# A two-layer decoder step on one core: row loads behind the barrier signal, an early gain load, and new orders on VectorE and TensorE

## What is computed

```
def rmsnorm(x, g):
    y = xf * lax.rsqrt(jnp.mean(xf * xf, axis=-1, keepdims=True) + RMS_EPS)
    return (y * g.astype(F32)).astype(x.dtype)
...
for layer in (0, 1):
    xp, xs = mixer(rmsnorm(xp, norm_mix[layer])), ...      # + residual
    xp = xp + hier_moe(rmsnorm(xp, norm_ffn[layer]), ...)  # y = sum of gate * expert(x) over two experts
    xs = xs + hier_moe(rmsnorm(xs, norm_ffn[layer]), ...)
y_prompt = rmsnorm(xp, norm_final)
y_sample = rmsnorm(xs, norm_final)
```

## Time and profile before

| | |
|---|---|
| median of the runs | 1451.35 us |
| the profiled execution's own time | 1448.17 us |
| its span, first to last instruction | 1446.4 us |
| mean granted TensorE clock | 0.943 |
| TensorE products busy | 1241.4 us, 86% |
| VectorE busy | 370.9 us, 26% |
| ScalarE busy | 246.5 us, 17% |
| GpSimd busy | 209.8 us, 15% |
| read from and written to HBM | 356.1 MB, 246 GB/s over the span |

### The profile page before, as it was taken

How to read it: one execution, slowest core, us unless ns; L and a number is a source line. 1 busy time by engine, 2 the same in 40 slices (tenths; PEclk the granted TensorE clock), 3 DMA queues, 4 the chain that set the end, 5 groups by cost and what they waited for, 6 DMA issues and landing times.

```text
span 1446.4 us, 16227 instructions
## 1 busy us (share of the span) xinstructions
PE 1241.4 (86%) x6273; PEld 658.5 (46%) x6273; DVE 370.9 (26%) x792; ACT 246.5 (17%) x571; POOL 209.8 (15%) x268
## 2 busy tenths in 40 slices
PE   6999998888789899877868999998879899878860
PEld 4765575556544533323324764445634533323320
DVE  4132003554310531111115400113610621111115
ACT  2000004653210301100003201014410301000001
POOL 2300002322200011111001000204810111111000
PEclk9999999999999999988998999999989999998985
DMA  8320524749957579999958130302156679999945
GB/s 278 100 49 18 214 106 140 215 150 351 359 201 301 225 267 418 419 420 420 414 222 285 59 113 8 131 0 82 45 205 279 240 283 420 419 419 419 415 182 182
DMA packets 104396, 342.58 MB, mean 237 GB/s; under 512 B 21534, under 2 KB 40162, under 8 KB 80506
## 3 DMA queue, kind: packets, MB, share of 16 engines
q1 hardware_dynamic: 89176, 305.47, 55.4%
q0 software_dynamic: 14848, 35.94, 6.9%
q10 hardware_dynamic: 290, 0.07, 0.0%
HBM read 320.08 MB, written 36.02 MB: 246 GB/s over the span
## 4 chain that ended last, share of the span: by engine, by line
PE 55%; SPq 16%; DMA 9%; DVE 8%; issue 4%; POOL 3%; ACT 3%; POOLq 2%; DVEq 0%; ACTq 0%
SPq L1037 10%; PE ps L1243 8%; PE ps L1747 8%; PE ps L1168 8%; SPq L1059 4%; PE ps L437 4%; DMA moe_gu<-in_moe_w_up 4%; PE ps L415 4%; PE ps L1698 4%; PE ps L1261 4%; DMA fox_arena<-in_cache_k 2%; PE ps L356 2%; DVE x L1582 1%; PE ps L695 1%; POOLq L340 1%
## 5 line engine op out<-in xcount | busy, mean ns | idle before, releaser
L1243 PE MATMUL ps<-moe_gu,rows 128*64 128x512 f32 x1024 | 246.7, 637 | 54.9 <-DMA moe_gu<-in_moe_w_up 51.6
L1243 PEld LDWEIGHTS ps<-moe_gu,rows 128*64 128x64 f32 x1024 | 81.7, 146 | 199.5 <-issue 191.8
L1747 PE MATMUL ps<-mwblk,turned 128*128 128x512 f32 x256 | 111.5, 593 | 2.2 <-DVE vaug L1938 1.5
L1168 PE MATMUL ps<-moe_gu,turned 128*128 128x512 f32 x256 | 110.3, 593 | 0.0
L1525 DVE TENSOR_TENSOR turned<-turned,ps 128x256 f32<-128x256 f32 x32 | 13.5, 421 | 305.5 <-ACT turned L1341 305.5
L1128 POOL DMA_INDIRECT expert_rows<-turned,moe_row x32 | 32.1, 1002 | 393.3 <-ACT turned L1351 385.7
L1261 PE MATMUL ps<-moe_wd,moe_rowsel 128*64 128x512 f32 x352 | 80.4, 598 | 2.3 <-ACT turned L1351 2.3
L1168 PEld LDWEIGHTS ps<-moe_gu,turned 128*128 128x128 f32 x256 | 48.6, 190 | 61.8 <-issue 61.0
L1747 PEld LDWEIGHTS ps<-mwblk,turned 128*128 128x128 f32 x256 | 48.0, 190 | 61.1 <-issue 57.4
L1341 ACT ACTIVATE turned<-ps 128x256 f32<-128x256 f32 x32 | 12.3, 383 | 302.5 <-PE ps L1243 302.5
L356 PE MATMUL ps<-turned,fox_arena 128*128 128x288 f32 x256 | 63.1, 407 | 0.0
(11 more groups left out here) (345 smaller groups left out, 1501.0 us busy)
## 6 DMA issues: line engine op xcount, KB each, us to landing
moe_gu<-in_moe_w_gate SPq DMA_DIRECT2D x56, 1024.0 KB, 22.1
moe_gu<-in_moe_w_up SPq DMA_DIRECT2D x56, 1024.0 KB, 23.9
moe_wd<-in_moe_w_down SPq DMA_DIRECT2D x44, 1024.0 KB, 23.2
rows<-in_moe_w_down SPq DMA_DIRECT2D x20, 1024.0 KB, 22.8
fox_arena<-in_cache_k SPq DMA_DIRECT2D x32, 512.0 KB, 7.9
fox_arena<-in_cache_v POOLq DMA_DIRECT2D x32, 512.0 KB, 9.5
fox_arena<-in_fox_w_in SPq DMA_DIRECT2D x6, 2048.0 KB, 10.3
mwblk<-in_mlstm_w_in SPq DMA_DIRECT2D x6, 2048.0 KB, 8.6
```

What stands on the lines that cost most here:

```text
L1168: mm = pe.matmul(ps[:, 2 * n + half, :], turned[:, c, n * P:(n + 1) * P], w[:, c, half * 512:half * 512 + 512], start=(c == 0), stop=(c == ...
L1243: mm = pe.matmul(ps[h, 2 + p % 2, :].rearrange("s (k f) -> s k f", k=2), xT[:, c, h], gu[s][:, half, :, c, :], start=(c == 0), stop=(c == ...
L1747: mm = pe.matmul(ps[:, m % 4, :], turned[:, c, n * P:(n + 1) * P], wblk[:, k % 3, c, :], start=(c == 0), stop=(c == KC - 1))
```

## The change

1. `scattered` becomes a semaphore outside the sets that are cleared, and SyncE's wait for it with the five row loads moves out of `sp_` into `late_`, which `run` calls after SyncE's drain and its increment of `together`, and before its wait for `cleared`.
2. The final gain is loaded by SyncE in layer 1's experts phase, after the last down weights and once pair 14's gate and up products are done, into a part of `gu[1]` that no row load writes. `finish` loads nothing; its VectorE waits for the gain first.
3. `aT` becomes two buffers by pair, and for the last pair TensorE does `turn_hidden(15)` ahead of `down(14)`, not after it.
4. `combine` issues one of its two instructions at a call, so that others can stand between. In the projection VectorE's order becomes the one in the diff, tile 3's and tile 4's adds being placed otherwise; in `finish` the mean of the tile before stands between the two adds.
5. TensorE in the projection issues seven idle products at the start in place of six, does `gates_half(0)` ahead of tile 3's flip as before, and puts tile 4's flip into the middle of `first_half(0)`.

```diff
-            aT = scratch[:, 0:2 * P].rearrange("p (m t) -> p m t", t=P)
+            aT = [scratch[:, k * 2 * P:(k + 1) * 2 * P].rearrange("p (m t) -> p m t", t=P) for k in range(2)]
...
+            last_gain.append(gu[1][:].rearrange("p h k c n -> p (h k c n)")[:, 2 * D:3 * D])
...
+                if layer == 1:
+                    sp.wait_ge(gu_done, STATIC - 1)
+                    sp.dma_start(last_gain[1], i["norm_final"].rearrange("(a d) -> a d", a=1).broadcast_to([P, D])).then_inc(gl_in, 16)
...
+            def late_(sp):
                 sp.wait_ge(scattered, 1)
                 for n in range(NT):
                     sp.dma_start(held[n][0:ROWS[n], :], y_dram[2 * n * P:2 * (n * P + ROWS[n]), :].rearrange("(p j) d -> p (j d)", j=2)
...
+                    if p == STATIC - 1:
+                        pe.wait_ge(at_kept, p)
+                        pe.wait_ge(a_ready, p + 1)
+                        turn_hidden(pe, p)
...
-                    pe.wait_ge(a_ready, p + 1)
-                    turn_hidden(pe, p)
+                    if p < STATIC - 1:
+                        pe.wait_ge(a_ready, p + 1)
+                        turn_hidden(pe, p)
...
             def pe_(pe):
-                idle_products(pe, 6, 5)
...
+                idle_products(pe, 7, 5)
+                for n in range(3):
+                    flip(pe, n)
+                    idle_products(pe, 1, 5)
+                pe.wait_ge(wg_in, 80)
+                pe.wait_ge(gained, 3)
+                gates_half(pe, 0)
+                flip(pe, 3)
+                pe.wait_ge(w_in[0], 16)
+                first_half(pe, 0, range(0, KC // 2))
+                flip(pe, L)
+                first_half(pe, 0, range(KC // 2, KC))
                 pe.wait_ge(gained, NT)
                 gates_half(pe, 1)
-                first_half(pe, 1)
+                first_half(pe, 1, range(KC))
...
+                for n in range(2):
+                    add_rows(n, 0)
+                    add_rows(n, 1)
                 mean(0)
-                combine(dve, 0, 2, combined)
+                add_rows(2, 0)
+                add_rows(2, 1)
                 mean(1)
+                add_rows(3, 0)
+                mean(2)
                 keep(0)
-                combine(dve, 0, 3, combined)
-                mean(2)
+                add_rows(3, 1)
                 keep(1)
                 mean(3)
                 keep(2)
-                combine(dve, 0, 4, combined)
+                add_rows(4, 0)
+                add_rows(4, 1)
                 keep(3)
...
             def dve_(dve):
+                dve.wait_ge(gl_in, 16)
                 for n in range(NT):
-                    combine(dve, 1, n, combined)
+                    combine(dve, 1, n, 0, combined)
                     if n:
                         mean(dve, n - 1)
-                    if n == 0:
-                        dve.wait_ge(gl_in, 16)
-                    else:
+                    combine(dve, 1, n, 1, combined)
+                    if n:
                         end(dve, n - 1)
...
                     eng.drain().then_inc(together, 1)
+                    if who == "sp" and "late" in phase:
+                        phase["late"](eng)
                     eng.wait_ge(cleared, n + 1)
```

More of the change, by code:

```diff
@@ L185, in trunk @@
         back = []
+        gl_in, last_gain = lasting("gl_in"), []
         def idle_products(pe, count, bank):
@@ L1260, in down @@
                             h = slice(half * SLOT, (half + 1) * SLOT)
-                            mm = pe.matmul(ps[h, 5 + n, :], aT[:, m, h], wd[s][:, half, m, n * 512:(n + 1) * 512],
+                            mm = pe.matmul(ps[h, 5 + n, :], aT[p % 2][:, m, h], wd[s][:, half, m, n * 512:(n + 1) * 512],
                                            start=(m == 0), stop=(m == 1))
@@ L1345, in keep_hidden @@
                 act.wait_ge(at_done, p + 1)
-                act.activation(aT[:], ps[:, 4, 0:2 * P].rearrange("p (m t) -> p m t", t=P), ACT.Copy).then_inc(at_kept, 1)
+                act.activation(aT[p % 2], ps[:, 4, 0:2 * P].rearrange("p (m t) -> p m t", t=P), ACT.Copy).then_inc(at_kept, 1)
             def keep_rows_act(act, p, s):
@@ L1567, in dve_, with combine @@
                             keep_rows_dve(dve, p, 0)
-            phases.append(dict(sp=sp_, pool=pool_, pe=pe_, act=act_, dve=dve_, clears="act"))
+            phases.append(dict(sp=sp_, pool=pool_, pe=pe_, act=act_, dve=dve_, clears="act", late=late_))
             mx.close()
-        def combine(dve, layer, n, combined):
+        def combine(dve, layer, n, j, combined):
             r = ROWS[n]
-            dve.wait_ge(back_in[layer][n], 16)
-            for j in range(2):
-                if j:
-                    dve.wait_ge(combined, 2 * n + 1)
-                dve.scalar_tensor_tensor(x[0:r, n, :], back[layer][n][0:r, j * D:(j + 1) * D], share[j][0:r, n:n + 1], x[0:r, n, :], ALU.mult, ALU.add
-                                         ).then_inc(combined, 1)
+            if j:
+                dve.wait_ge(combined, 2 * n + 1)
+            else:
+                dve.wait_ge(back_in[layer][n], 16)
+            dve.scalar_tensor_tensor(x[0:r, n, :], back[layer][n][0:r, j * D:(j + 1) * D], share[j][0:r, n:n + 1], x[0:r, n, :], ALU.mult, ALU.add
+                                     ).then_inc(combined, 1)
         def mlstm_project(qT, kT, knat, vaug, og, nat, carryb, C, qs, ws, tri01, negg_dram, small):
@@ L1768, in gates_half, with first_half, flip @@
                     mm.then_inc(g_done, 1)
-            def first_half(pe, half):
-                for c in range(KC):
+            def first_half(pe, half, chunks):
+                for c in chunks:
                     mm = pe.matmul(ps[:, 4 + half, 0:HT], wblk[:, 0, c, 0:P], turned[:, c, half * HT:(half + 1) * HT],
                                    start=(c == 0), stop=(c == KC - 1))
-                if half:
+                if half and c == KC - 1:
                     mm.then_inc(k_done, 1)
-            def pe_(pe):
-                idle_products(pe, 6, 5)
-                for n, r in enumerate(ROWS):
-                    pe.wait_ge(scaled, n + 1)
-                    if n >= 2:
-                        pe.wait_ge(gained, n - 1)
-                    for c in range(KC):
-                        mm = pe.transpose(ps2[:, n % 2, c * P:c * P + r], rows[0:r, n, c:D:KC], ident[0:r, 0:r])
-                    mm.then_inc(flipped, 1)
-                    if n < 3:
-                        idle_products(pe, 1, 5)
-                    if n == 2:
-                        pe.wait_ge(wg_in, 80)
-                        pe.wait_ge(gained, 3)
-                        gates_half(pe, 0)
-                    if n == 3:
-                        pe.wait_ge(w_in[0], 16)
-                        first_half(pe, 0)
+            def flip(pe, n):
+                r = ROWS[n]
+                pe.wait_ge(scaled, n + 1)
+                if n >= 2:
+                    pe.wait_ge(gained, n - 1)
+                for c in range(KC):
+                    mm = pe.transpose(ps2[:, n % 2, c * P:c * P + r], rows[0:r, n, c:D:KC], ident[0:r, 0:r])
+                mm.then_inc(flipped, 1)
+            def pe_(pe):
+                idle_products(pe, 7, 5)
[10 more added lines that the diff above has]
+                first_half(pe, 0, range(KC // 2, KC))
                 pe.wait_ge(gained, NT)
                 gates_half(pe, 1)
-                first_half(pe, 1)
+                first_half(pe, 1, range(KC))
                 for g in range(1, 8):
@@ L2413, in finish @@
             L = NT - 1
-            sb("f_held", [P, 2 * NT, D], where=fin)
-            gl = sb("gl", [P, D], where=fin)
+            sb("f_held", [P, 2 * NT + 1, D], where=fin)
+            gl = last_gain[1]
             combined = sem("f_combined")
-            gl_in, squared, meaned, rooted, ended, y_out = (sem("gl_in"), sem("f_squared"), sem("f_meaned"), sem("f_rooted"),
+            squared, meaned, rooted, ended, y_out = (sem("f_squared"), sem("f_meaned"), sem("f_rooted"),
                                                             sem("f_ended"), sem("y_final"))
             def sp_(sp):
-                sp.dma_start(gl[:], i["norm_final"].rearrange("(a d) -> a d", a=1).broadcast_to([P, D])).then_inc(gl_in, 16)
                 for n in range(NT):
```

6 lines of the change are left out of this document (3 added, 3 removed).

## The result

The changed kernel took 1439.06 us (median of 20 runs, 1431.81 to 1448.98) against 1451.66 of the kernel before (20 runs, 1446.47 to 1458.44): 12.6 us less, a ratio of 0.9914 with a 95% interval of 0.9898 to 0.9930. The forecast was 15.2 less and 1436.2. Between executions of one kernel the time follows TensorE's clock: among these twenty the slowest had a mean granted clock of 0.937 and the fastest 0.948.

A forecast was written before the change was run, and what follows sets the result against it. Chains of waits at the experts' end, projection (TensorE) and last phase (the gain, then VectorE) bound it; 11.6 + 1.8 + 0.3 + 1.5 = 15.2 off the median 1451.35 gave 1436.2 us, own range 1433.5 to 1439, wide range 1431 to 1442.

The forecast's parts named there:

- The release: Barrier behind each layer's last scatter: signalling ahead of the row loads brings release 2.7 us behind the scatter, 3.1 earlier.
- rival B: Release doesn't move, because GpSimd's drain ends with something unseen: 1438.5 us, chance 0.08.
- The last phase, 11.6: Last phase: early release, early gain and means between adds end VectorE's work at 1431.4, saving 11.6 us.
- Four of these vanish, since the second add (1.28) now covers them: Last phase: four of five VectorE waits of 0.66 us for GpSimd's power disappear, 20.2 becoming 17.6.
- the sign of being right: Last phase: some 20.4 us from VectorE's first add to its last end, no idle time over 1 us.
- The last pair, 1.8 and 0.3: Experts' end: turning ahead of `down(14)` starts the last down products earlier, 1.8 us in layer 1, 0.3 in layer 0.
- The projection, 1.5: Projection behind layer 0: gate products start at 778.0, the phase ends 1.5 us earlier, bounds 0 and 3.2.
- The sum: Whole kernel: savings of 11.6, 1.8, 0.3 and 1.5 add up to 15.2 us.
- rival A: Layer 1's tail keeps its place through later pair 15 weights or a clock fall, losing the 1.8: 1438.0 us, chance 0.14.
- C: Last phase: row loads bound it, tiles 2 to 4 landing 3 to 4 us late: 1440 us, chance 0.05.
- E: DMA serves SyncE's waiting transfers side by side, delaying rows and last down weights: 6.4 us slower, 1457.8, chance 0.02.
- a sign of being wrong: Listed signs: rows releasing tiles 2 to 4, VectorE releasing a gate product, or GpSimd's drain over 3 us.

The follow-up runs named there:

- signal_last: The changed kernel with SyncE signalling the barrier after issuing the row loads, as before: 1441.24 us, ratio 0.9923 to the kernel before.
- adds_in_row: The changed kernel with both adds of a tile in a row in the last phase, the mean behind them: 1439.72 us, ratio 0.9911 to the kernel before.
- end_lagged: The changed kernel with each tile's end issued one tile later in the last phase: 1436.22 us, ratio 0.9894 to the kernel before.
- tail_filled: The changed kernel with the old projection order, last-phase ends one tile later, and one idle product on each side of the last turning: 1433.46 us, ratio 0.9870.
- bridged: The changed kernel with three idle products for one behind tile 2's flip and one ahead of tile 4's in the projection: 1437.55 us, ratio 0.9905.
- bridged_lagged: The changed kernel with bridged's extra idle products in the projection and last-phase ends issued one tile later: 1439.00 us, ratio 0.9922.
- gain_late: The changed kernel with the final gain loaded at the start of the last phase again: 1448.73 us, ratio 0.9974 to the kernel before.

## Why the prediction was right or wrong

The direction and the wide range (1431 to 1442) held; the size was 2.6 too large, and 1439.06 lies at the very edge of the forecast's own range, 1433.5 to 1439. That it came this near is in part luck, as errors of both signs add up below. By its own steps:

**The release.** Right. The drain behind layer 0's last scatter began at 757.21 and took 2.67; the rows' landings stayed (4.86 for tile 0). The last phase gains 1.7 us by it, where rival B's difference had been put at 2.0. In the projection nothing is shown to have been gained by it (signal_last).

**The last phase, 11.6.** Mis-sized by 1.4. The step that failed is "Four of these vanish, since the second add (1.28) now covers them". The waits shrank from 0.66 to 0.43 only, because GpSimd's power is held up by VectorE's add: 4 x 0.43 = 1.7, less some 0.06 a tile, as a tile now takes 4.23 us and before took 4.52. Both adds_in_row and end_lagged bear this out. The Trainium skill has this as a rule (SBUF — State Buffer, Who interferes with whom): VectorE and GpSimd share a port pair that is locked for a whole instruction, and a VectorE instruction with two SBUF inputs takes it against a GpSimd one that reads SBUF. The rows agree, with 1.57 us against 0.54, and with 0.54 beside `keep`, whose second input isn't in SBUF. The prediction should have priced it, and the trace of before had the price, in the first power of the projection, which ran beside VectorE's adds and which the prediction took at 0.6:

```profile
766.05 2.60 DVE L1582 SCALAR_TENSOR_TENSOR x<-moe_gu,share,x 128x1024 f32<-128x1024 f32 x2
766.22 1.53 POOL L1692 TENSOR_TENSOR rstd<-ms,cst 128x1 f32<-128x1 f32 x1 [14.30 <-DVE ms L1860]
```

The start, put at +4.7 behind the issue, came at +5.0, but tile 1's adds began at +7.5, as forecast. From VectorE's first add to its last end it took 21.6 us, where 20.4 had been named as the sign of being right.

**The last pair, 1.8 and 0.3.** The mechanism is right in both layers: the end goes to the landing of the weights (products 21.7 us behind their issue in layer 0 in all ten traces of the new order, 22.3 in layer 1 where the clock stays). The size in layer 1 is 1.85 when the clock stays, as forecast, and 0.65 when it falls. Of those ten (tail_filled left aside), five had 3.65 us for pair 14's products and five 5.3 to 5.35; I had given the fall, together with late weights, 0.14. The sentence that failed is that no idle stretch over 1 us is left and so the clock stays: two pauses of 1.0 and 0.9 us with half a microsecond of transposes between them are enough for it to fall in half of the executions. Layer 0 was mis-sized the other way: 0.3 against the trace that I had, but 2.0 and 2.1 against the two later traces of the old order there, in which TensorE paused for 1.96 and 2.16 us instead of 1.19 and the clock fell. Three traces don't say how often it does there.

**The projection, 1.5.** Its parts were right where they were about order: gate products at +23.3 forecast and +22.5 to +24.0 found in the seven traces of the new order, `m0T` behind the first block as the releaser in the six of them with the early signal, a gap of 1.2 us ahead of tile 4's flip where 1.1 was worked out. Wrong was that only the wait was priced and not what TensorE's clock does behind it. The six traces of the new order with the early signal (bridged and bridged_lagged left aside) gave 46.1, 45.9, 44.1, 45.3, 42.6 and 42.2 us, a mean of 44.4, against 44.5 and 44.1 in the two traces with the old release and order. So on average nothing was won and not 1.5, with anything from 2.3 won to 1.5 lost in one execution.

With the old order and the early release it was 42.9, 42.2 and 43.8, on average 43.0. The place differs as well. The clock falls around the gate products in both orders (5.78 us for them in two of the seven traces of the new one, of which signal_last's is one, and 4.71 and 5.15 in two of five of the old one). Behind the pause ahead of tile 4's flip, where the new order has cut the first products in two, it fell in four of seven (3.2 to 3.9 us for the eight products behind the flip, 2.21 otherwise), while the sixteen in a row of the old order took 4.05 in all five. So the cut is likely to cost a little, but three traces (43.0) against six with the early release (44.4) and overlapping intervals of the times (0.9900 and 0.9914) don't prove it.

**The sum.** 10.2 + 1.2 (mean of 1.85 and 0.65) + 0.3 to 2.1 + 0 = 11.7 to 13.5, and 12.6 was measured. What the last phase (1.4), layer 1's pair (0.6) and the projection (1.5) fell short by, layer 0's pair gave back in part (up to 1.8), for a reason that the forecast didn't have. Half of rival A, the fall of the clock, happened in five traces of ten; the last weights came when forecast. B, C and E didn't happen. Release came 2.7 us behind the last scatter. In the last phase tiles 1 to 4 were never waited for. In the projection of the changed kernel VectorE does wait for tile 3's rows, 0.51 us, which by the forecast's list is a sign of being wrong; but they landed at +13.1, against +12.7 before, and it is the new order that asks for them earlier than the +14.0 that the forecast had. Last, gain_late rules E out where it would cost most, since the last weights take 21.1 us from issue to landing with the gain behind them or without, and the gain lands 1.3 us behind them. That is also what the Trainium skill says (DMA: Bandwidth & Descriptors, Queues, rings and completion order): on one DMA engine a queue's descriptors are consumed in ring order. The 16.4 us at which the gain lands, whenever it is issued behind the rows, agree with it.

## What to carry to other kernels

A small transfer that a whole phase waits for goes ahead of the large ones in the queue, not behind them: that was worth 8.9 us here, more than any new order of the engines' work. When a wait is to be hidden under another engine's work, look in the trace for the waited instruction beside that work first; its time alone isn't its time there. And where TensorE pauses, price the clock behind the pause, from several profiles, since one profile shows one draw.

## What the runs showed of the hardware that I had not expected

- I hadn't expected it, though the skill's rule above says it: GpSimd's power on 128 x 1 took 0.54 to 0.56 us with VectorE still or at a `keep` with an input in PSUM, and 1.5 to 1.6 while a float32 VectorE add of 1.28 us with both large inputs in SBUF ran; it ended 0.4 us behind that instruction.
- TensorE's granted clock fell to 1.2 GHz behind pauses of 1.2 to 2.1 us in some executions and not in others (42.2 and 46.1 us for one stretch of the same kernel; in end_lagged it stayed behind 2.21 us), and behind two pauses of about 1 us in five traces of ten. Ahead of pair 14's products in the old order it fell in all five places where the pause was 1.96 us or more, and not behind 1.19.
- A transfer of 512 KB issued 3 us earlier into the same queue landed at the same time, 16.4 us behind the queue's first row load.
